# adaLN products with the weight tile stationary and the two conditions moving

## The chip, the cores and the metric

The kernel runs on one core of one Trainium2 chip. The metric is the device time of one execution in microseconds (us). Engines: PE (TensorE), DVE (VectorE), ACT (ScalarE), POOL (GpSimd) and SP (SyncE, which issues the loads of weights here). In the profile PEld stands for PE's weight loads (LDWEIGHTS) and PE for its matmuls.

## What is computed

One inference step through two trunk layers of a diffusion backbone, for 128 context tokens and 256 latent tokens of 1024 channels. Context tokens are modulated by one condition, latent tokens by another. Cut to what the change touches:

```python
mod = (jax.nn.silu(cond) @ w_ada + b_ada)[:, None, :]
sh1, sc1, gt1, sh2, sc2, gt2 = jnp.split(mod, 6, axis=-1)
h = rms_norm(x, g_mix) * (1 + sc1) + sh1
p = h @ w_in
# attention, gated linear attention (GLA) and RWKV-7 mixers on p, merged by gates
x = x + gt1 * (merged @ w_out)
h2 = rms_norm(x, g_ffn) * (1 + sc2) + sh2
x = x + gt2 * ((jax.nn.silu(gu[..., :D_FF]) * gu[..., D_FF:]) @ w_ffn_out)
```

w_ada is 1024 x 6144 in each layer, and cond is c_ctx for the context tokens and c for the latent ones. All is fp32; the large projections split their operands in a high and a low part and multiply these (L547 to L549, L1045 to L1047), the adaLN products do not.

## The kernel before

The channels lie on the 128 partitions and the 384 tokens (T) along the free axis, so that modulation is wanted as columns: mod is [128, layer, 48, 2], 48 blocks of 128 channels by two conditions. For each layer the phases are: norm and input projections, attention, GLA, RWKV, then merging, output projection and FFN. Between phases stands a barrier of all engines.

Each engine's program is written out by hand, and its instructions run in that order; engines wait for each other by semaphores. Beside the main line of a phase PE runs *side work*: a generator, side_steps, walks a plan (side_plan) of work items, and `fill(n)` runs its next n steps at the point where it stands in PE's program. Items are "ada" (adaLN: 256 of the 6144 columns of w_ada), "gate" (a 128-column gate projection, L603) and "po" (a branch's output projection, L609). An "ada" item is two steps, "po" two, "gate" four. finish(l, k) runs what is left of a plan at the end of its phase.

- Layer 0's ada items 0 to 7 run before everything else, by themselves. Items 8 to 15 of each layer stand in the plan of attention, 16 to 23 in that of GLA, and items 0 to 7 of layer 1 in the plan of layer 0's RWKV phase.
- Side work uses two PSUM banks in turn. fill_room makes PE wait until the item two places back has been emptied, by ACT (key "A") or by DVE (key "V").
- An ada item has cond (scond, 128 channels x 2 conditions for each of 8 blocks k) stationary and w_ada moving. It leaves 2 rows of 256 in PSUM; ACT copies them to a row buffer, modrow, of which there are two; turn_mod, which stands behind the item that follows, turns each row buffer into columns by two transposes; DVE adds the bias b_ada and writes mod:

```python
ins = pe.matmul(b[0:2, 0:256], scond[:, :, k], w[:, k, :], start=k == 0, stop=k == KD - 1)
...
A(modrow[0:2, j % 2, :], bank(*t)[0:2, 0:256], ACT.Copy).then_inc(*empties(*t))
...
ins = turn(b[:, 2 * i:2 * i + 2], modrow[0:2, j % 2, 128 * i:128 * i + 128])
```

- ACT and DVE empty side work in side_work(tag), called ahead of each main item: it takes all side items that PE's program finished before the item with that tag.
- The weights of all items and projections come through a ring of three buffers of 1 MB in one order (order), loaded by SP. A buffer is loaded again when its last user is done.

Names in the profile: L598 are the ada products, L499 all transposes (those of modrow have bank<-cst,modrow), L1162 ACT's copy to modrow, L1585 DVE's addition to mod, L532 the sum of squares for a norm, L713 attention's scores, L700 its output, L787 the 12 products of a GLA level, L921, L932 and L944 the narrow products of a step of the RWKV scan, L1126 and L1128 POOL's inverses.

Of the kernel before, what the change touches and what calls it, by code (L numbers as in the profile page):

```python
# [7 lines left out]
KD = D // 128  # L8
# [78 lines left out]
def step_kernel(nc, x_prompt, x_sample, cache_k, cache_v, state_gla, state_rwkv, c, c_ctx,  # L87
# [8 lines left out]
    with ExitStack() as ctx:  # L96
        offset = {}

        def sb(name, shape):
            offset[name] = nc.sbuf_base  # L100
            return ctx.enter_context(nc.sbuf_tensor(name, shape, fp32))
# [12 lines left out]
        gate = sb("gate", [128, KD, T])  # L114
# [7 lines left out]
        cst = sb("cst", [128, NCONST])  # L122
        par = sb("par", [128, L, 128])
        mod = sb("mod", [128, L, 48, 2])
        modrow = sb("modrow", [2, 2, 256])
        gtmp = sb("gtmp", [128, 2, T])
        sc1 = sb("sc1", [128, KD, 2])
        sc2 = sb("sc2", [128, KD, 2])
# [144 lines left out]
        def filled(*tag):  # L273

            return place[tag][1] + 1
# [5 lines left out]
        def emptied(*tag):  # L281

            side, n = place[tag]
            row = fills if side else items
            key = row[n][0]
            return (fill_freed if side else freed)[key], sum(1 for k, _ in row[:n + 1] if k == key)
# [180 lines left out]
        def _(pe):  # L467
# [12 lines left out]
            def fill_room():  # L480
                n = len(fills)
                return emptied(*fills[n - 2][1]) if n >= 2 else (consts_in, 16)

            def fill_item(key, *tag):
                fills.append((key, tag))
                place[tag] = 1, len(fills) - 1
                return bank(*tag)
# [9 lines left out]
            def turn(out, in_, rows=None):  # L497
                rows = rows or slice(0, in_.shape[0])
                return pe.transpose(out, in_, ident[rows, rows])  # L499
# [73 lines left out]
            h_parts = tiles(h_hi, KD), tiles(h_lo, KD)  # L573

            def turn_mod(l, j):

                pe.wait_ge(*emptied("ada", l, j))
                pe.wait_ge(*fill_room())
                b = fill_item("V", "modT", l, j)  # L580
                for i in range(2):
                    ins = turn(b[:, 2 * i:2 * i + 2], modrow[0:2, j % 2, 128 * i:128 * i + 128])
                ins.then_inc(fill_ready, 1)
                finished.append(("modT", l, j))

            def side_steps(plan):

                for n, work in enumerate(plan):
                    kind, l, j = work[0], work[1], work[-1]
                    last_of_chunk = all(chunk(later) != chunk(work) for later in plan[n + 1:])  # L590
                    pe.wait_ge(*arrived(*chunk(work)))
                    w = weights(*chunk(work))
                    pe.wait_ge(*fill_room())
                    b = fill_item("V" if kind == "po" else "A", *work)
                    if kind == "ada":

                        for k in range(KD):
                            ins = pe.matmul(b[0:2, 0:256], scond[:, :, k], w[:, k, :], start=k == 0, stop=k == KD - 1)  # L598
                            if k == 3:
                                yield  # L600
                    elif kind == "gate":
                        for k in range(KD):
                            ins = pe.matmul(b[:, 0:T], w[:, k, 128 * (j % 2):128 * (j % 2) + 128], h[:, k, :], start=k == 0, stop=k == KD - 1)  # L603
                            if k % 2 and k < KD - 1:
                                yield
                    else:
                        src = (pa[:, 0:4, :], pb[:, 4:8, :])[work[2]]
                        for k in range(4):
                            ins = pe.matmul(b[:, 0:T], w[:, k, 128 * (j % 4):128 * (j % 4) + 128], src[:, k, :], start=k == 0, stop=k == 3)  # L609
                            if k == 1:  # L610
                                yield
                    ins.then_inc(fill_ready, 1)
                    finished.append(work)
                    if last_of_chunk:
                        fill_used(*chunk(work))
                    if n and plan[n - 1][0] == "ada":
                        turn_mod(*plan[n - 1][1:])
                    yield
                if plan[-1][0] == "ada":
                    turn_mod(*plan[-1][1:])  # L620

            side = [iter(())]

# [524 lines left out]
        def _(act):  # L1148
            step, tells, empties, last, before = counting("A")
            A = act.activation  # L1150
            told_ada = []

            def side_work(*tag):

                for t in before(*tag):
                    if t[0] == "ada":
                        l, j = t[1:]
                        if len(told_ada) >= 2:
                            act.wait_ge(fill_ready, filled("modT", *told_ada[-2]))
                        told_ada.append((l, j))  # L1160
                        act.wait_ge(fill_ready, filled(*t))
                        A(modrow[0:2, j % 2, :], bank(*t)[0:2, 0:256], ACT.Copy).then_inc(*empties(*t))  # L1162
                        continue
                    kind, l, br, j = t
                    if br == 0:
                        place = mg[:, j, :]
                    elif br == 1:
                        place = gtmp[:, j % 2, :]
                        if j >= 2:
                            act.wait_ge(S["branch_merged"], told("branch_merged", l, j - 1))  # L1170
                    else:
                        place = last_gates[j]
                        act.wait_ge(fill_ready, filled("po", l, 1, 7))
                    act.wait_ge(fill_ready, filled(*t))
                    A(place, bank(*t)[:, 0:T], ACT.Sigmoid).then_inc(*empties(*t))
# [397 lines left out]
        def _(dve):  # L1573
# [3 lines left out]
            def side_work(*tag):  # L1577

                for t in before(*tag):
                    l, j = t[1], t[-1]  # L1580
                    dve.wait_ge(fill_ready, filled(*t))
                    b = bank(*t)
                    if t[0] == "modT":
                        bias = par[:, l, ROW["b_ada"] + 2 * j:ROW["b_ada"] + 2 * j + 2].unsqueeze(2).to_broadcast([128, 2, 2])
                        tt(mod[:, l, 2 * j:2 * j + 2, :], b[:, 0:4].rearrange("p (a b) -> p a b", a=2), bias, add).then_inc(*empties(*t))  # L1585
                        continue

                    dve.wait_ge(*emptied("gate", *t[1:]))
                    if t[2] == 0:
                        tt(mg[:, j, :], b[:, 0:T], mg[:, j, :], mult).then_inc(*empties(*t))  # L1590
                    else:
                        tt(gtmp[:, j % 2, :], b[:, 0:T], gtmp[:, j % 2, :], mult).then_inc(*empties(*t))
                        dve.wait_ge(*last())
                        tt(mg[:, j, :], mg[:, j, :], gtmp[:, j % 2, :], add).then_inc(*tells("branch_merged"))
# [548 lines left out]
```

## Time and profile before

| | us |
|---|---|
| median of 3 runs | 2234.6 (2234.24 to 2237.12) |
| the profiled execution | 2236.58 |
| its span, first to last instruction | 2234.8 |
| PE busy | 1952.0 (87%) |
| DVE, ACT, POOL busy | 1055.9, 838.4, 283.0 |
| mean granted clock of PE | 0.923 of full speed |

The profile is of one execution. Rows of groups give the line, engine, operation, output<-inputs, shapes and the number of records, then the busy time of all and the mean of one in ns. A fp32 matmul of this kernel leaves two records (and two weight loads), a transpose one.
### The profile page before, as it was taken

What the parts mean: (1) busy time and instruction counts of PE and PEld (TensorE: products, weight loads), DVE (VectorE), ACT (ScalarE), POOL (GpSimd) and SP (SyncE); (2) the same over time, 40 slices, a digit from 0 to 9 for tenths busy, and PEclk for the clock granted to TensorE, in tenths of its full rate; (3) what the DMA queues carried; (4) which work ended last, traced back from release to release, by engine and by line L of the source; (5) the groups of instructions that cost most, each with busy time, mean ns of one, the idle gap of its engine ahead of it and who ended that gap; (6) DMA issues with size and microseconds to landing.
All of it is one profiled execution on the core that took longest, in us unless ns stands there. A gap on an engine that the chain in (4) does not pass through costs nothing.

```text
span 2234.8 us, 32380 instructions
## 1 busy us (share of the span) xinstructions
PE 1952.0 (87%) x13395; PEld 1551.7 (69%) x13395; DVE 1055.9 (47%) x1939; ACT 838.4 (38%) x1408; POOL 283.0 (13%) x550
## 2 busy tenths in 40 slices
PE   6899998967985798999989989897787668899998
PEld 2799445634554598999979965464444557799998
DVE  0336427754565544343342544384466645533433
ACT  1533533253333535333253345324324334533322
POOL 2000000015555000000000000000553520000000
PEclk9999999978996799999999999998887569999999
DMA  7433333202130143443433423323101003344342
GB/s 255 132 116 104 100 113 123 95 24 76 58 114 20 33 151 94 121 125 105 128 112 122 125 82 114 107 92 99 57 2 57 2 1 102 111 114 132 107 119 85
DMA packets 267769, 214.07 MB, mean 96 GB/s; under 512 B 7209, under 2 KB 259400, under 8 KB 267368
## 3 DMA queue, kind: packets, MB, share of 16 engines
q1 hardware_dynamic: 264640, 204.39, 30.1%
q0 software_dynamic: 2736, 7.54, 1.1%
q8 instruction: 107, 1.75, 0.3%
q14 instruction: 38, 0.31, 0.0%
q10 hardware_dynamic: 248, 0.07, 0.0%
HBM read 209.10 MB, written 2.88 MB: 95 GB/s over the span
## 4 chain that ended last, share of the span: by engine, by line
PE 70%; DVE 11%; ACT 7%; POOL 7%; issue 3%; DMA 1%; DVEq 0%; ACTq 0%; POOLq 0%
PE bank L547 10%; PE bank L548 10%; PE bank L549 10%; PE bank L603 8%; PE bank L598 7%; POOL cst L1128 4%; POOL lora L1126 3%; PE bank L1047 3%; PE bank L1046 3%; PE bank L1045 3%; PE bank L609 2%; PE bank L787 2%; PE bank L499 1%; ACT h L1192 1%; PE bank L834 1%
## 5 line engine op out<-in xcount | busy, mean ns | idle before, releaser
L549 PE MATMUL bank<-scr_rounded 128*128 128x384 f32 (+1 forms) x1312 | 442.0, 337 | 0.0
L603 PE MATMUL bank<-h,ring 128*128 128x384 f32 x640 | 249.0, 538 | 21.8 <-DVEq L337 17.9
L547 PE MATMUL bank<-scr_rounded 128*128 128x384 f32 x672 | 230.2, 343 | 26.0 <-DVE scr_rounded L1605 24.2
L549 PEld LDWEIGHTS bank<-scr_rounded 128*128 128x128 f32 (+1 forms) x1312 | 247.9, 189 | 1.0
L548 PE MATMUL bank<-scr_rounded 128*128 128x384 f32 x672 | 227.7, 339 | 0.0
L1600 DVE TENSOR_TENSOR scr_rounded<-ring,scr_rounded 128x2048 fp32r<-128x2048 f32 (+1 forms) x64 | 136.1, 2126 | 177.6 <-ACT scr_rounded L1183 176.8
L547 PE MATMUL bank<-scr_rounded,gate_rounded 128*128 128x384 f32 (+1 forms) x640 | 214.6, 335 | 4.4 <-DVE scr_rounded L1600 4.4
L548 PE MATMUL bank<-scr_rounded,gate_rounded 128*128 128x384 f32 (+1 forms) x640 | 214.3, 335 | 0.0
L603 PEld LDWEIGHTS bank<-h,ring 128*128 128x128 f32 x640 | 126.5, 207 | 119.4 <-issue 54.8
L598 PE MATMUL bank<-ring,scond 128*2 128x256 f32 x768 | 182.1, 391 | 19.5 <-DVE mg L1590 6.0
L1600 DVE TENSOR_TENSOR scr_rounded<-ring,gate_rounded 128x2048 fp32r<-128x2048 f32 (+3 forms) x64 | 130.2, 2034 | 106.0 <-ACT gate_rounded L1183 105.4
L1183 ACT ACTIVATE scr_rounded<-ring 128x2048 fp32r<-128x2048 f32 (+1 forms) x64 | 114.0, 1781 | 145.2 <-PE bank L549 74.8
L1183 ACT ACTIVATE gate_rounded<-ring 128x2048 fp32r<-128x2048 f32 (+3 forms) x64 | 109.2, 1707 | 146.4 <-PE bank L549 85.7
L547 PEld LDWEIGHTS bank<-scr_rounded 128*128 128x128 f32 x672 | 128.9, 192 | 32.0 <-issue 26.5
L598 PEld LDWEIGHTS bank<-ring,scond 128*2 128x2 f32 x768 | 62.7, 87 | 124.2 <-issue 40.4
L1128 POOL TENSOR_TENSOR cst<-cst,lora 128x30 f32<-128x30 f32 (+14 forms) x240 | 128.2, 534 | 18.8
L548 PEld LDWEIGHTS bank<-scr_rounded 128*128 128x128 f32 x672 | 128.8, 192 | 0.3
L547 PEld LDWEIGHTS bank<-scr_rounded,gate_rounded 128*128 128x128 f32 (+1 forms) x640 | 119.4, 187 | 6.0 <-DVE scr_rounded L1600 5.1
L1126 POOL TENSOR_TENSOR lora<-cst 128x30 f32<-128x30 f32 (+14 forms) x240 | 120.1, 500 | 18.2
L548 PEld LDWEIGHTS bank<-scr_rounded,gate_rounded 128*128 128x128 f32 (+1 forms) x640 | 119.3, 186 | 1.0
L2097 DVE TENSOR_TENSOR arena<-bank,arena 128x384 f32<-128x384 f32 x44 | 24.5, 558 | 177.1 <-PE bank L549 175.6
L609 PE MATMUL bank<-arena,ring 128*128 128x384 f32 x256 | 94.2, 511 | 2.8 <-DVE mod L1585 1.6
(358 smaller groups left out, 3253.7 us busy)
## 6 DMA issues: line engine op xcount, KB each, us to landing
ring<-in_w_in_dram SPq DMA_DIRECT2D x56, 1024.0 KB, 5.3
ring<-in_w_ada_dram SPq DMA_DIRECT2D x48, 1024.0 KB, 5.3
ring<-in_w_ffn_in_dram SPq DMA_DIRECT2D x88, 512.0 KB, 5.1
ring<-in_w_ffn_out_dram SPq DMA_DIRECT2D x32, 704.0 KB, 4.6
ring<-in_w_out_dram SPq DMA_DIRECT2D x8, 1024.0 KB, 5.1
ring<-in_w_po_a_dram SPq DMA_DIRECT2D x4, 1024.0 KB, 6.3
ring<-in_w_po_b_dram SPq DMA_DIRECT2D x4, 1024.0 KB, 5.4
ring<-in_w_po_c_dram SPq DMA_DIRECT2D x4, 1024.0 KB, 6.3
```

The source lines that it names most:

```text
L547: pe.matmul(o, w_hi[:, k, :], right[0][k], start=k == 0, stop=False)
L548: pe.matmul(o, w_hi[:, k, :], right[1][k], start=False, stop=False)
L549: ins = pe.matmul(o, w_lo[:, k, :], right[0][k], start=False, stop=k == nk - 1)
L598: ins = pe.matmul(b[0:2, 0:256], scond[:, :, k], w[:, k, :], start=k == 0, stop=k == KD - 1)
L603: ins = pe.matmul(b[:, 0:T], w[:, k, 128 * (j % 2):128 * (j % 2) + 128], h[:, k, :], start=k == 0, stop=k == KD - 1)
L609: ins = pe.matmul(b[:, 0:T], w[:, k, 128 * (j % 4):128 * (j % 4) + 128], src[:, k, :], start=k == 0, stop=k == 3)
L1045: pe.matmul(b[:, 0:T], w_hi[:, k, :], ff_hi[n], start=n == 0, stop=False)
L1046: pe.matmul(b[:, 0:T], w_hi[:, k, :], ff_lo[n], start=False, stop=False)
L1126: gp.tensor_tensor(t, W[:, i + 1:32, i:i + 1].to_broadcast([128, more, i]), over(W[:, i, 0:i], more), mult).then_inc(*step())
L1128: gp.tensor_tensor(W[:, i + 1:32, 0:i], W[:, i + 1:32, 0:i], t, add).then_inc(*(step() if i < 30 else tells("rw_inv")))
L1183: A(shaped(whi[m % 2], name, j), weights(l, name, j), ACT.Copy).then_inc(*tells("w_hi"))
L1600: tt(shaped(wlo[m % 2], name, j), weights(l, name, j), value(shaped(whi[m % 2], name, j)), sub).then_inc(*tells("w_lo"))
```

## The change

The weight tile becomes the stationary operand and the condition the moving one. Each item is then 2 x 8 instructions, which leave the two blocks of 128 channels as columns in PSUM, in the layout that the transposes had left there. modrow, turn_mod and ACT's copy are gone; the item's bank is emptied by DVE's addition, which is the same instruction as before. The step of the generator now ends after the first block of 128 channels, so that an item is still two steps of equal length.

```diff
-        modrow = sb("modrow", [2, 2, 256])
...
-            def turn_mod(l, j):
-
-                pe.wait_ge(*emptied("ada", l, j))
-                pe.wait_ge(*fill_room())
-                b = fill_item("V", "modT", l, j)
-                for i in range(2):
-                    ins = turn(b[:, 2 * i:2 * i + 2], modrow[0:2, j % 2, 128 * i:128 * i + 128])
-                ins.then_inc(fill_ready, 1)
-                finished.append(("modT", l, j))
...
-                    b = fill_item("V" if kind == "po" else "A", *work)
+                    b = fill_item("A" if kind == "gate" else "V", *work)
                     if kind == "ada":
 
-                        for k in range(KD):
-                            ins = pe.matmul(b[0:2, 0:256], scond[:, :, k], w[:, k, :], start=k == 0, stop=k == KD - 1)
-                            if k == 3:
+                        for i in range(2):
+                            for k in range(KD):
+                                ins = pe.matmul(b[:, 2 * i:2 * i + 2], w[:, k, 128 * i:128 * i + 128], scond[:, :, k], start=k == 0, stop=k == KD - 1)
+                            if i == 0:
                                 yield
...
-                    if n and plan[n - 1][0] == "ada":
-                        turn_mod(*plan[n - 1][1:])
                     yield
-                if plan[-1][0] == "ada":
-                    turn_mod(*plan[-1][1:])
...
-                    if t[0] == "ada":
-                        l, j = t[1:]
-                        if len(told_ada) >= 2:
-                            act.wait_ge(fill_ready, filled("modT", *told_ada[-2]))
-                        told_ada.append((l, j))
-                        act.wait_ge(fill_ready, filled(*t))
-                        A(modrow[0:2, j % 2, :], bank(*t)[0:2, 0:256], ACT.Copy).then_inc(*empties(*t))
-                        continue
...
-                    if t[0] == "modT":
+                    if t[0] == "ada":
                         bias = par[:, l, ROW["b_ada"] + 2 * j:ROW["b_ada"] + 2 * j + 2].unsqueeze(2).to_broadcast([128, 2, 2])
```

The order of PE's instructions at the start of the program (L598 are the ada products, dve_emptied_fill and act_emptied_fill the waits for a bank of side work), before:

```order
L598 MATMUL bank<-ring,scond 2x256 [waits consts_in,w_arrived1]
L598 MATMUL bank<-ring,scond 2x256 x7
L499 MATMUL bank<-cst,modrow 128x2 [waits act_emptied_fill]
L499 MATMUL bank<-cst,modrow 128x2
L598 MATMUL bank<-ring,scond 2x256 [waits act_emptied_fill,w_arrived2]
L598 MATMUL bank<-ring,scond 2x256 x7
L499 MATMUL bank<-cst,modrow 128x2 [waits dve_emptied_fill,act_emptied_fill]
L499 MATMUL bank<-cst,modrow 128x2
```

and after the change, where the products stand in L588:

```order
L588 MATMUL bank<-scond,ring 128x2 [waits consts_in,w_arrived1]
L588 MATMUL bank<-scond,ring 128x2 x15
L588 MATMUL bank<-scond,ring 128x2 [waits dve_emptied_fill,w_arrived2]
L588 MATMUL bank<-scond,ring 128x2 x15
L588 MATMUL bank<-scond,ring 128x2 [waits dve_emptied_fill,w_arrived0]
L588 MATMUL bank<-scond,ring 128x2 x15
```

Items now follow each other on PE with no transposes between them, and the wait for ACT has become one for DVE.

PE in the first levels of GLA in layer 0 (L787 are the 12 products of a level), before:

```order
L598 MATMUL bank<-ring,scond 2x256 [waits act_emptied_fill,w_arrived2]
L598 MATMUL bank<-ring,scond 2x256 x7
L499 MATMUL bank<-cst,modrow 128x2 [waits dve_emptied_fill,act_emptied_fill]
L499 MATMUL bank<-cst,modrow 128x2
L787 MATMUL bank<-scr 128x128 [waits dve_emptied,gla_z]
L787 MATMUL bank<-scr 128x128 x5
L787 MATMUL bank<-scr 128x128 [waits dve_emptied]
L787 MATMUL bank<-scr 128x128 x5
L598 MATMUL bank<-ring,scond 2x256 [waits act_emptied_fill,w_arrived0]
L598 MATMUL bank<-ring,scond 2x256 x7
```

and after, with the level's products in L773:

```order
L588 MATMUL bank<-scond,ring 128x2 [waits dve_emptied_fill,w_arrived2]
L588 MATMUL bank<-scond,ring 128x2 x15
L773 MATMUL bank<-scr 128x128 [waits dve_emptied,gla_z]
L773 MATMUL bank<-scr 128x128 x5
L773 MATMUL bank<-scr 128x128 [waits dve_emptied]
L773 MATMUL bank<-scr 128x128 x5
L588 MATMUL bank<-scond,ring 128x2 [waits dve_emptied_fill,w_arrived0]
L588 MATMUL bank<-scond,ring 128x2 x15
```

Each item keeps its level; an item is 16 instructions in place of 8 and two transposes.

## Rows read from the trace of the kernel before

**Rows 1.** The page: busy time by engine, and the chain that ended last.
```profile
PE 1952.0 (87%) x13395; PEld 1551.7 (69%) x13395; DVE 1055.9 (47%) x1939; ACT 838.4 (38%) x1408; POOL 283.0 (13%) x550
...
PE 70%; DVE 11%; ACT 7%; POOL 7%; issue 3%; DMA 1%; DVEq 0%; ACTq 0%; POOLq 0%
PE bank L547 10%; PE bank L548 10%; PE bank L549 10%; PE bank L603 8%; PE bank L598 7%; POOL cst L1128 4%; POOL lora L1126 3%; PE bank L1047 3%; PE bank L1046 3%; PE bank L1045 3%; PE bank L609 2%; PE bank L787 2%; PE bank L499 1%; ACT h L1192 1%; PE bank L834 1%
```

**Rows 2.** Groups by line: busy us, mean ns | idle before, releasers.
```profile
L598 PE MATMUL bank<-ring,scond 128*2 128x256 f32 x768 | 182.1, 391 | 19.5 <-DVE mg L1590 6.0 <-DVEq L337 5.0 <-issue 4.4
...
L1162 ACT ACTIVATE modrow<-bank 2x256 f32<-2x256 f32 x48 | 17.9, 372 | 120.6 <-PE bank L598 117.2 <-DVE scr L1906 3.4
```

**Rows 3.** Chain of waits from the start: start us, us, what.
```profile
38.63 3.63 PE bank L598 x16
42.34 0.38 ACT modrow L1162
42.85 3.63 PE bank L598 x16
...
60.28 5.18 PE bank L532 x16
```

**Rows 4.** Timeline of PE, three runs of transposes: start us, us, engine, line.
```profile
14.98 4.82 PE L499 MATMUL bank<-cst,mg 128*128 128x128 f32 x24
...
467.04 0.72 PE L499 MATMUL bank<-cst,scr 64*128 64x64 f32 x8
...
2225.27 2.81 PE L499 MATMUL bank<-cst,x 128*128 128x128 f32 x24 [0.93 <-DVEq L337]
```

**Rows 5.** Stretches of first products: PE, PEld, DVE, ACT, POOL, PEclk, DMA share, GB/s.
```profile
24.30:29.30 5.00, 4.99 (x12) 1.49 (x13) 0.00 (x0) 0.00 (x0) 0.00 (x0) 0.50 1.05 333
29.40:59.30 29.90, 27.54 (x131) 10.75 (x129) 0.97 (x6) 2.67 (x8) 0.00 (x0) 1.00 0.76 245
```

**Rows 6.** Timeline of PE in the levels of GLA, layer 0.
```profile
367.75 3.62 PE L598 MATMUL bank<-ring,scond 128*2 128x256 f32 x16
371.30 0.28 PE L499 MATMUL bank<-cst,modrow 2*128 2x2 f32 x2
371.51 1.61 PE L787 MATMUL bank<-scr 64*128 64x128 f32 x24
373.05 3.62 PE L598 MATMUL bank<-ring,scond 128*2 128x256 f32 x16
...
389.04 2.82 PE L609 MATMUL bank<-arena,ring 128*128 128x384 f32 x8 [0.81 <-DVE mod L1585]
391.79 1.61 PE L787 MATMUL bank<-scr 64*128 64x128 f32 x24
393.33 2.85 PE L609 MATMUL bank<-arena,ring 128*128 128x384 f32 x8
```

**Rows 7.** RWKV scans of layer 0: timeline of PE, then stretches.
```profile
625.51 1.89 PE L598 MATMUL bank<-ring,scond 128*2 128x256 f32 x8
627.33 0.73 PE L932 MATMUL bank<-cst,scr 64*64 64x64 f32 x16
...
688.06 1.15 PE L932 MATMUL bank<-cst,scr 64*64 64x64 f32 x16 [1.84 <-issue]
...
624.50:654.10 29.60, 27.65 (x227) 13.61 (x226) 14.19 (x50) 5.42 (x19) 26.07 (x46) 1.00 0.69 214
684.40:702.60 18.20, 11.98 (x150) 9.11 (x148) 13.00 (x45) 4.38 (x14) 12.71 (x28) 0.50 0.00 1
```

**Rows 8.** Timeline of PE and DVE in a pair of attention blocks.
```profile
253.57 0.92 PE L713 MATMUL bank<-scr,arena 64*128 64x384 f32 x4
254.42 2.85 PE L603 MATMUL bank<-h,ring 128*128 128x384 f32 x8
256.55 0.42 DVE L1738 TENSOR_SCALAR scr<-scr,small 128x384 f32<-128x384 f32 x1
257.10 0.82 PE L499 MATMUL bank<-cst,scr 128*128 128x128 f32 x6
```

**Rows 9.** Stretch of GLA levels without an ada item, same columns.
```profile
388.00:410.00 22.00, 21.19 (x158) 13.85 (x156) 21.03 (x44) 4.88 (x7) 0.00 (x0) 1.00 0.15 49
```

More of the change, by code:

```diff
@@ L1150, in _ @@
             A = act.activation
-            told_ada = []
             def side_work(*tag):
                 for t in before(*tag):
-                    if t[0] == "ada":
-                        l, j = t[1:]
-                        if len(told_ada) >= 2:
-                            act.wait_ge(fill_ready, filled("modT", *told_ada[-2]))
-                        told_ada.append((l, j))
-                        act.wait_ge(fill_ready, filled(*t))
-                        A(modrow[0:2, j % 2, :], bank(*t)[0:2, 0:256], ACT.Copy).then_inc(*empties(*t))
-                        continue
                     kind, l, br, j = t
```

## The prediction, made before the changed kernel ran

> **What bounds the kernel now.** I read the page's shares and its chain first: TensorE (PE) is busy for 87% of the span and makes 70% of the chain that ended last; the adaLN products alone (L598) are 7% of that chain [rows 1]. So what happens to PE's time counts wherever the chain runs through PE, and I then looked at the four places in which these products run, for what ends last there.
>
> The groups by line give unit times [rows 2]. Each instruction in fp32 leaves two records. An adaLN item (8 instructions) is 16 records. The timeline gives an item as one piece of 3.61 to 3.62 us, its two transposes of modrow behind it (0.28 us shown, 0.21 to the next start) [rows 6]. Start to start, a half item (8 records) takes 1.82 us [rows 7], so about 216 ns a record once 0.1 us for the break is taken off. 48 items are 48 x 3.83 = 184 us of PE.
>
> - *Start (24.3 to 60 us).* Nothing but these products runs. PE waits between items for ScalarE's copy to modrow (0.37 us each [rows 2]), so an item is 4.2 us from start to start [rows 3].
> - *Attention.* In a pair of blocks PE runs scores, a piece of side work, transposes. VectorE and ScalarE need until 256.97 for scores begun at 253.57, and the transposes start at 257.10 [rows 8]: with a gate piece of 2.85 us PE and the others just meet, with an adaLN item of 3.62 us PE is the later by some 0.7 us.
> - *GLA.* Each level is L787 (1.61 us, 1.54 to the next start) and one piece: 5.3 us with an adaLN item, 4.3 us with a 2.85 us piece [rows 6]. In the levels with the shorter pieces VectorE is busy 21.03 of 22 us [rows 9]. So about 4.2 us is the floor of a level, whatever PE saves.
> - *RWKV scans of layer 0.* Narrow products (64 columns) alternate with half items of 1.89 us [rows 7].
>
> **The change part by part.** An item becomes 16 instructions, 32 records, each with a stationary tile of 128x128 and 2 moving columns. Gone are 96 transposes, 48 copies on ScalarE and the wait for them. VectorE's 48 additions stay as they are and now empty the product itself; a wait for them stands where PE waited for ScalarE. Behind that wait on PE are all later products of the stage; VectorE reaches it before the PE needs the bank again in the orders shown, and where it was late (0.81 us at 389.0 [rows 6]) it was late before. I cost this at nothing, up to 0.8 us a time if that cover fails. The ring's 1 MB loads keep their places; with DMA at a share of 0.76 in the first stage [rows 5] a shorter item could wait for its weights there, see the first rival.
>
> *A record at full clock.* With 2 columns there is nothing to hide the loading of 128 columns of weights. The nearest row is the run of eight transposes that move 64 columns against a 128-column stationary tile [rows 4]: 0.72 us, of which a lone record is 0.28, so (0.72 - 0.28) / 7 = 63 ns from start to start. The upper bound is that of 128 moving columns, (2.81 - 0.28) / 23 = 110 ns [rows 4], the lower one half of it, 55 ns, since 64 columns could fill no more than that. I take 63, since that row is limited by the load: an item is 32 x 63 + two breaks of 0.1 = 2.2 us against 3.83, 1.6 less. The Trainium skill (TensorE: Matmul & The Clock Gate, section "LDWEIGHTS (loading the stationary operand)") gives columns / 1.2, so 107 ns for 128 columns: by it an item would be an estimated 3.6 us and nearly all of the gain at full clock would be gone. The 63 ns row is shorter than that rule, so the row decides.
>
> *A record at half clock.* Some 57 of the 63 ns should be the load itself and double with the clock: 115 to 120 ns, I take 115. The upper bound is the slow run of 128-column transposes at 15 us, 24 in 4.82 us, 200 ns each [rows 4]. An item is 32 x 115 + 0.2 = 3.9 us: as much as the old one at full clock.
>
> *Which clock it is.* This decides everything. A new record moves 2 columns where an old one moves 256: 216 ns x 2/256, under 2 ns in 63. The rows show what held the clock. In the RWKV scans with a half item between the narrow products the granted clock is 1.00 (2.4 GHz); the same scans without anything between them run at 0.50 (1.2 GHz), though PE is busy for 12.0 of 18.2 us and weights are being loaded for half of it (9.1 us) [rows 7]. The old items at 24.3 us began at 0.50 and went on at 1.00 [rows 5], though their stationary tile has only 2 columns: moving columns raised it, not the width of the tile. Items of 2 moving columns should therefore look idle, and I expect the clock to fall to 1.2 GHz behind each run of them, and to stay there until wide products have run for some us. The Trainium skill (same page, "Part 1: The HAM clock gate") says that the gate follows how busy PE has been and does not say whether loading weights counts; that is the first rival.
>
> The sum, at the expected clock:
>
> 1. Start: 256 records x 115 ns = 29.4 us against 35.8 (24.3 to 60.1): -6. The 16 records of L532 behind them (5.18 us at full clock [rows 3]) begin at half, 640 ns each; 7.5 us if the clock rises after some ten of them: +2.5. Sum -3.5, bounds -6 and -1.
> 2. Attention, each layer: the opening fill is 48 records, about 40 at full clock and then half, 4.2 us against 5.3, and the ten records of L657 behind it (384 moving columns, 0.32 us each as in L532 [rows 3]) at half clock cost 2 to 3 more: +1. Of six later items some three leave the clock up and gain 1.1 each (VectorE allows no more: 3.4 us from score to transpose); three bring it down, so that the next scores, transposes and gate piece (0.92, 0.82 and 2.85 us [rows 8]) run partly at half, +2 to +3 each. -3.3 + 6.6 + 1 = +4 a layer, bounds -3 and +11.
> 3. GLA, each layer: a level at full clock 4.2 against 5.3, at half 3.9 + 3.2 = 7.1, so -1.1 or +1.8. First item -1, its following L499/L773 at half +0.8, three levels in a row one fast and two slow +2.5, first wide level after them at half +2; then a lone level -1, two in a row +0.8, the output products L798/L802 begun at half +2, last item -1: +5 a layer, bounds -5 and +12.
> 4. RWKV, layer 0: 16 half items at 1.95 against 1.83, +2; the narrow products between them at half as at 688 us, where 16 records of L932 take 1.15 us against 0.73 [rows 7]: +0.9 a scan step, 4.5 steps, +4; two steps until the clock is back, +2; transposes gone, -2. +6, bounds -2 and +10.
>
> -3.5 + 8 + 10 + 6 = +20.5. The profiled execution took 2236.58 us with a span of 2234.8 (1.8 us around it); the median of the three timed runs is 2234.6, 2.0 below it. Put on the median: 2255.
>
> **The rivals.** *The clock holds* (weight loads count as activity, or the pieces around suffice). Then each item is 2.2 us. Start: the first us are at half clock all the same, afterwards the ring limits: 1 MB at 333 GB/s [rows 5], about 3.1 us an item, -10 in all. Attention: -1.1 for six items and -2 for the opening, -8.5 a layer. GLA: eight items at -1.1, -9 a layer (VectorE's 4.2 us is the bound). RWKV: 8 items of which VectorE and POOL (7% of the chain, L1126 and L1128 [rows 1]) let some 1.0 each through, -8. -10 - 17 - 18 - 8 = -53, from 2234.6: 2182. For it: no row shows weights loaded for long without moving columns, so that this is excluded by none. Against it: the scans at 0.50 with loads half the time [rows 7]. It decides from the point at which a run of items leaves the granted clock at 1.00.
>
> *The change saves nothing on PE*: a load of 128 fp32 rows takes the upper bound of 110 ns at both clocks. An item is 3.7 us, as before, and the clock falls all the same: the sum gets the fast items' gains back, +8: about 2262. The skill's rule above would end here.
>
> *The falls are cheap*: the clock comes back within one piece, since every second piece is wide. Attention and GLA come to nothing or -3 a layer, RWKV +2, start -3.5: 2230 to 2237, about 2234, no measurable difference.
>
> **How the numbers follow.** The forecast has 0.57, its own range 2238 to 2275 (nearly the ends of its terms, which won't all fall together). The clock holds: 0.28, 2172 to 2200. Nothing saved: 0.05. Cheap falls: 0.10. For 8 in 10 the range must reach into the first rival: 2172 to 2275. A measurement of this kernel can tell some 0.2% (4.5 us) from no change. Faster by more: 0.28 and a little of the cheap falls, 0.30. Within: 0.08. Slower: 0.62.
>
> **What would show it.** PEclk (slices and stretches) at 0.5 in 25 to 60 us and under 0.9 in the GLA levels with adaLN items; a piece of 32 records of 3.7 us there and of 2.1 us where the clock is still up; the gate and score pieces behind items lengthened. VectorE's additions to mod wait for the products themselves, and the 48 copies of L1162 (17.9 us [rows 2]) are gone. If PEclk is 1.00 in all adaLN runs, the reading of the clock is wrong and the first rival's sum holds; if 32 records take over 3.4 us at 1.00, the price of the load is wrong.

## The result, and the profile after

The changed kernel takes 2386.1 us (median; 2365.7 to 2390.1) against 2234.4: 1.065 times the time of before, 95% interval 1.062 to 1.069. It is 152 us slower; the forecast had been 20 slower, and the range ended at 2275. In this document a ratio and its interval leave out runs over 1.5% above a kernel's fastest, which only two programs had.

The page of the changed kernel: busy time, and the granted clock of PE in 40 slices of the span.

```profile
PE 2114.8 (89%) x14067; PEld 1806.2 (76%) x14067; DVE 1057.8 (44%) x1939; ACT 823.2 (34%) x1360; POOL 282.8 (12%) x550
...
PEclk6799888758587589999999988867688757999999
...
PE bank L588 11%; PE bank L546 10%; PE bank L548 10%; PE bank L547 10%; PE bank L593 9%; POOL cst L1114 3%; POOL lora L1112 3%; PE bank L1032 3%; PE bank L1031 3%; PE bank L1033 3%; PE bank L773 2%; PE bank L599 2%; ACT h L1169 1%; PE bank L498 1%; PE bank L699 1%
```

PE is busy for 163 us more than in [rows 1], PEld for 254 us more, DVE for 2 more. In the kernel before the same clock row reads:

```profile
PEclk9999999978996799999999999998887569999999
```

The adaLN products have gone from 7% of the chain to 11%. The groups by line, of the changed kernel and then of before (busy us, mean ns | idle before):

```profile
L588 PE MATMUL bank<-scond,ring 128*128 128x2 f32 x1536 | 274.9, 314 | 14.3 <-DVE mg L1567 6.0 <-DVEq L336 5.0 <-issue 3.3
L593 PE MATMUL bank<-h,ring 128*128 128x384 f32 x640 | 271.2, 577 | 20.7 <-DVEq L336 17.9 <-DMA ring<-in_w_in_dram 2.9
L773 PE MATMUL bank<-scr 64*128 64x128 f32 x672 | 61.0, 345 | 0.0
L1562 DVE TENSOR_TENSOR mod<-bank,par 128x4 f32<-128x4 f32 x48 | 7.7, 161 | 163.8 <-PE bank L588 163.4
```

```profile
L603 PE MATMUL bank<-h,ring 128*128 128x384 f32 x640 | 249.0, 538 | 21.8 <-DVEq L337 17.9 <-DMA ring<-in_w_in_dram 2.2 <-ACT mg L1175 0.9
L787 PE MATMUL bank<-scr 64*128 64x128 f32 x672 | 45.0, 280 | 0.0
```

The adaLN products themselves cost 275 us of busy time against 182 [rows 2], and products that the change doesn't touch became dearer too: a gate record takes 577 ns in place of 538 on average, a record of a GLA level 345 in place of 280. The stretches of the start answer to [rows 5] (PE, PEld, DVE, ACT, POOL, PEclk, DMA share, GB/s):

```profile
24.30:29.30 5.00, 5.00 (x25) 5.00 (x25) 0.00 (x0) 0.00 (x0) 0.00 (x0) 0.50 0.85 267
29.40:59.30 29.90, 29.90 (x141) 29.90 (x142) 0.81 (x5) 0.00 (x0) 0.00 (x0) 0.50 0.46 147
```

Here PE loads weights without a pause, and the granted clock is 0.50 (1.2 GHz) where it was 1.00. 141 records in 29.9 us are 212 ns each. The timeline of PE in the levels of GLA answers to [rows 6]:

```profile
414.08 2.93 PE L773 MATMUL bank<-scr 64*128 64x128 f32 x24
416.94 6.99 PE L588 MATMUL bank<-scond,ring 128*128 128x2 f32 x32
423.86 2.94 PE L773 MATMUL bank<-scr 64*128 64x128 f32 x24
426.72 6.99 PE L588 MATMUL bank<-scond,ring 128*128 128x2 f32 x32
433.64 2.94 PE L773 MATMUL bank<-scr 64*128 64x128 f32 x24
436.50 3.96 PE L599 MATMUL bank<-arena,ring 128*128 128x384 f32 x8
440.39 1.61 PE L773 MATMUL bank<-scr 64*128 64x128 f32 x24
```

A level with an item is 9.8 us from start to start (416.94 to 426.72) against 5.3: the item 6.9 in place of 3.6, the level's own products 2.9 in place of 1.6. Inside the first wide piece behind them the clock comes back, and the next level is at its old 1.61 us.

From the times at which the same PE record of either trace starts, the stages compare like this:

| Stretch (layer) | before, us | after, us | longer by |
|---|---|---|---|
| start to L532/L531 (0) | 60.1 | 77.9 | 17.8 |
| to attention's L657/L643, with the opening fill (0) | 167.6 | 171.6 | 4.0 |
| to GLA's L736/L722 (0) | 111.7 | 127.1 | 15.4 |
| GLA (0) | 123.0 | 159.9 | 36.9 |
| RWKV, to the first L547/L546 behind it (0) | 321.8 | 344.3 | 22.5 |
| to attention's L657/L643 (1) | 528.0 | 534.6 | 6.6 |
| attention (1) | 111.9 | 125.1 | 13.2 |
| GLA (1) | 123.3 | 159.8 | 36.5 |
| the rest, with no adaLN item in it | 687.4 | 687.9 | 0.5 |

All of the loss lies in the stretches that hold adaLN items. Adding up PE's records of both traces, each from its start to the next start and without idle time, gives the second split: the items (in the kernel before with the transposes of modrow) went from 190 to 271 us, all other records from 1762 to 1844, PE's idle time shrank by 9. So about half of the loss is the items' own length, and half is their neighbours, which took longer at half clock.

What a record costs is read from the same starts: inside items the distance is 112 ns where the granted clock is 1.00 and 213 ns where it is 0.50. Of 1489 such distances 918 lay wholly or partly at half clock.

### The profile page after: what moved, and what is told of

Read it like the earlier page. It is cut to its first block, busy times and chain, and to the rows that moved or that the text cites. A ratio compares the mean times of both kernels' runs of the same rounds, so it can differ in the third digit from the quotient of the medians.

```text
span 2388.2 us, 33583 instructions
## 1 busy us (share of the span) xinstructions
PE 2114.8 (89%) x14067; PEld 1806.2 (76%) x14067; DVE 1057.8 (44%) x1939; ACT 823.2 (34%) x1360; POOL 282.8 (12%) x550
## 4 chain that ended last, share of the span: by engine, by line
PE 73%; DVE 9%; POOL 7%; ACT 6%; issue 3%; DMA 1%; DVEq 0%; ACTq 0%; POOLq 0%
PE bank L588 11%; PE bank L546 10%; PE bank L548 10%; PE bank L547 10%; PE bank L593 9%; POOL cst L1114 3%; POOL lora L1112 3%; PE bank L1032 3%; PE bank L1031 3%; PE bank L1033 3%; PE bank L773 2%; PE bank L599 2%; ACT h L1169 1%; PE bank L498 1%; PE bank L699 1%
## 5 line engine op out<-in xcount | busy, mean ns | idle before, releaser
L588 PEld LDWEIGHTS bank<-scond,ring 128*128 128x128 f32 x1536 | 271.9, 278 | 27.3 <-issue 24.9
L593 PE MATMUL bank<-h,ring 128*128 128x384 f32 x640 | 271.2, 577 | 20.7 <-DVEq L336 17.9
L588 PE MATMUL bank<-scond,ring 128*128 128x2 f32 x1536 | 274.9, 314 | 14.3 <-DVE mg L1567 6.0
L546 PE MATMUL bank<-scr_rounded 128*128 128x384 f32 x672 | 230.3, 343 | 26.1 <-DVE scr_rounded L1582 24.2
L593 PEld LDWEIGHTS bank<-h,ring 128*128 128x128 f32 x640 | 138.1, 226 | 131.3 <-issue 74.8
L547 PE MATMUL bank<-scr_rounded 128*128 128x384 f32 x672 | 227.6, 339 | 0.0
L546 PE MATMUL bank<-scr_rounded,gate_rounded 128*128 128x384 f32 (+1 forms) x640 | 215.3, 336 | 4.4 <-DVE scr_rounded L1577 4.4
L547 PE MATMUL bank<-scr_rounded,gate_rounded 128*128 128x384 f32 (+1 forms) x640 | 215.1, 336 | 0.0
L546 PEld LDWEIGHTS bank<-scr_rounded 128*128 128x128 f32 x672 | 128.7, 192 | 32.4 <-issue 26.5
L547 PEld LDWEIGHTS bank<-scr_rounded 128*128 128x128 f32 x672 | 128.8, 192 | 0.3
L546 PEld LDWEIGHTS bank<-scr_rounded,gate_rounded 128*128 128x128 f32 (+1 forms) x640 | 120.0, 188 | 6.0 <-DVE scr_rounded L1577 5.1
L547 PEld LDWEIGHTS bank<-scr_rounded,gate_rounded 128*128 128x128 f32 (+1 forms) x640 | 119.9, 187 | 1.0
```

The costliest lines, as they stand in the source:

```text
L546: pe.matmul(o, w_hi[:, k, :], right[0][k], start=k == 0, stop=False)
L547: pe.matmul(o, w_hi[:, k, :], right[1][k], start=False, stop=False)
L588: ins = pe.matmul(b[:, 2 * i:2 * i + 2], w[:, k, 128 * i:128 * i + 128], scond[:, :, k], start=k == 0, stop=k == KD - 1)
```

## The experiments

Theory A, formed on these two traces: a record is limited by the load of its 128 fp32 columns, at 112 ns at full and 213 ns at half clock, so an item at full clock is no shorter than the old one; and the clock falls because of the few moving columns. Rivals: the clock falls through the weight loads or the waits (B), load and moving add up (C), the neighbours' half clock is most of the loss (D), the phases' losses hang together (E). Two came up later, on the price of a load (G) and on a wait (H).

### 128 moving columns

In all experiments of this kind scond is repeated by an access pattern with step 0, so that m columns move; DVE reads two of them. Everything else is the changed kernel.

```diff
-ins = pe.matmul(b[:, 2 * i:2 * i + 2], w[:, k, 128 * i:128 * i + 128], scond[:, :, k], ...)
+m = 128
+ins = pe.matmul(b[:, m * i:m * i + m].rearrange("p (a b) -> p a b", b=2), w[:, k, 128 * i:128 * i + 128],
+                scond[:, :, k].unsqueeze(1).to_broadcast([128, m // 2, 2]), ...)
```

> The changed kernel, but with 128 moving columns in each adaLN product (the two conditions repeated 64 times; only two of the columns are used), weights still stationary. Theory A (a record is limited by the load of 128 fp32 columns, 111 ns at full clock and 213 at half, and the clock falls because so few columns move): 128 columns move in the shadow of the load, a record stays at 110 to 112 ns, an item at 3.6 us, and PEclk is 1.00 in the adaLN stretches; then only the transposes and the copy's wait are gone, 4.6 us at the start and some 0.2 us for each other item where PE is the later: about 2221 us, 2212 to 2232. Rival B (the clock falls through the many weight loads of 128 columns, or the waits, not through the moving columns): PEclk stays at 0.5 in the start and the time at 2365 to 2390. Rival C (load and moving do not overlap): about 218 ns a record at full clock, an item 7 us, time 2350 or more.

Measured: 2227.1 us, 0.9965 of before (0.9952 to 0.9977), within the range expected. 64 times as many columns go through PE, and it takes 159 us less than the changed kernel. The stretches of the start, and two levels of GLA:

```profile
24.30:29.30 5.00, 5.00 (x27) 5.00 (x27) 0.00 (x0) 0.00 (x0) 0.00 (x0) 0.57 1.05 331
29.40:59.30 29.90, 29.90 (x245) 28.18 (x244) 4.33 (x14) 3.19 (x2) 0.00 (x0) 1.00 0.87 278
```

```profile
366.59 1.61 PE L774 MATMUL bank<-scr 64*128 64x128 f32 x24
368.13 3.84 PE L589 MATMUL bank<-scond,ring 128*128 128x128 f32 x32
371.90 1.61 PE L774 MATMUL bank<-scr 64*128 64x128 f32 x24
```

The clock is at 1.00 with the same stationary tiles, the same number of loads and the same waits: rival B falls. A record is 112 ns as with 2 moving columns at full clock, so the 128 columns move wholly beside the load: rival C falls. An item is 3.77 us (368.13 to 371.90). A level is 5.31 us against 5.29 of before (one old item and the two transposes): in GLA the form gains nothing even at full clock. What it does gain is the start, where no copy by ACT is waited for (5 us at the norm), and 3 us in attention of each layer.

### 256 moving columns

> The same with 256 moving columns. It lengthens the items about as the half clock does, but should leave the clock up. Theory A: 213 to 216 ns a record at PEclk 1.00 in all adaLN runs, an item 6.9 us, neighbours at their lengths of before; so +19 us at the start and 3 us for each of the 40 other items where PE is the later, about +130 us in all: 2350 to 2375 us, and by as much as it stays below 2386 the neighbours at half clock had cost more. If the neighbours' half clock were the greater part of the loss (rival D), this kernel would be below 2320. Rival B: PEclk 0.5 here too, 400 ns a record and over 2450 us.

Measured: 2387.1 us, 1.068 of before (1.066 to 1.069). The granted clock of the start is that of before, and the neighbours have their old length:

```profile
29.40:59.30 29.90, 29.90 (x138) 26.02 (x137) 0.65 (x4) 0.00 (x0) 0.00 (x0) 1.00 0.43 141
```

```profile
425.94 1.61 PE L774 MATMUL bank<-scr 64*128 64x128 f32 x24
427.48 7.25 PE L589 MATMUL bank<-scond,ring 128*128 128x256 f32 x32
434.67 1.61 PE L774 MATMUL bank<-scr 64*128 64x128 f32 x24
```

A record is 218 ns: now the moving of 256 columns is the limit. At full clock an item is 7.2 us, some 3.4 more than the old one with its transposes (3.83), and 48 x 3.4 = 163 us, less what PE waited for in before, is what the kernel lost. The expectation was 12 to 37 us too low, since it took 3 us an item and only where PE is the later. It also was a poor test of D: here all 48 items are long, in the changed kernel only those at half clock. That the two totals agree is chance; the changed kernel's split into 81 us of items and 82 of neighbours rests on the traces' records alone. By the same adding up the kernel with 256 columns has 349 us of items and 1764 of all other records, which is 159 and 2 more than before. What this run shows is that items twice as long cost their full length nearly everywhere, so PE's side work is on the path in all four stages.

### 2 moving columns in the start alone, and in GLA alone

```diff
+m = 2 if l == 0 and j < 8 else 128      # the start
+m = 2 if 16 <= j < 24 else 128          # GLA
```

> 128 moving columns everywhere but in the first eight items, which run alone at the start with 2 as in the changed kernel. Theory A: PEclk 0.50 through 23 to 78 us, 256 records at 213 ns in 54.7 us, and nothing lost behind the norm: 2221 + 24 = about 2245 us, 2235 to 2255. Rival E: more than 30 us above m128.

Measured: 2252.7 us, 25.6 above the kernel with 128 columns, 24 expected. The granted clock of the start:

```profile
24.30:77.00 52.70, 52.70 (x249) 52.70 (x249) 1.14 (x7) 3.19 (x2) 0.00 (x0) 0.50 0.52 167
```

> 128 moving columns everywhere but in the items of GLA (16 to 23 of each layer), which have 2 as in the changed kernel. Theory A: the loss is local to the phase; GLA is 36.6 us longer in each layer than before, as in the changed kernel, and PEclk returns to 1.00 behind it: 2221 + 2 x 38 = about 2297 us, 2285 to 2310. Rival E (the losses of the phases hang together through the weight ring and the side work's plan): less than half of that, or some of it in attention and RWKV.

Measured: 2265.7 us for the two shorter of four runs, 1.013 of before (1.012 to 1.015). That is 39 above the kernel with 128 columns and 19 below the expected range. The four runs were 2265, 2267, 2307 and 2307 us, so the same program lost 39 or 80 us. The longer runs had the lower mean granted clock, 0.885 against 0.897; why a run gets the one or the other was not settled. The trace is of one of the short runs. In it GLA is 22.5 and 20.9 us longer than before in the two layers, where the changed kernel's was 36.9 and 36.5: the expectation had the changed kernel's loss here, and this trace shows little more than half of it.

Rival E is answered by the stages of the two traces. With 2 columns in the start alone, the start is 24 us longer than in the second trace of the kernel with 128 columns (from the last experiment), the stretch from there to attention 3, and each other stage lies within 1 us of it. With 2 columns in GLA alone, each other stage lies within 3 us of the first trace of that kernel. So the losses of the phases don't hang together, beyond the 3 us of products that follow the start while the clock is still down.

### 64 and 32 moving columns

> As the run with 128 moving columns (weights stationary, 128 columns), but 64 move. Theory A: the record's price stays 111 ns at full and 213 at half clock; the time then tells only the clock. Half the moving columns for the same time should let it fall in some of the item runs: 2235 to 2300 us, PEclk in the start between 0.5 and 1.0. Rival B (columns don't matter for the clock below 256): as 128 columns, 2227 us. Rival C (load and moving add up): shorter by 50 ns a record than with 128.

> The same with 32 moving columns. Theory A: the record still takes 111 or 213 ns; the clock stays at 0.50 in the start as with 2 columns, 256 records in 54.7 us, and the whole time is 2350 to 2390 us. If 32 columns already hold the clock, 2227 us; the two between them place where the clock is lost.

Measured: 2296.0 us with 64 columns (1.026 of before, 1.024 to 1.028) and 2348.4 with 32 (1.049, 1.047 to 1.051; 2 us under the expected range). The time with 64 columns is within its range, but the clock of the start was expected between 0.5 and 1.0 and is 0.50. The second stretch of the start, first with 64 and then with 32 columns:

```profile
29.40:59.30 29.90, 29.90 (x142) 29.90 (x142) 0.81 (x5) 0.00 (x0) 0.00 (x0) 0.50 0.46 147
```

```profile
29.40:59.30 29.90, 29.90 (x142) 29.90 (x142) 0.81 (x5) 0.00 (x0) 0.00 (x0) 0.50 0.44 142
```

In both, records have the distances of the changed kernel, 112 ns at full and 213 at half clock; only their share at half clock differs: 918 of 1489 with 2 columns, 666 with 32, 471 with 64, 61 with 128. The time rises with that share: 2386, 2348, 2296, 2227 us. So up to 128 the number of moving columns acts on the time through the clock alone. The places differ too: with 64 columns the start is 17.6 us longer than before, as with 2, and RWKV 12.5, but GLA only 2.5 and 7.1.

### Half of the stationary columns

```diff
+m = 64
+for n, k in enumerate([0, *range(KD)]):
+    c = 64 if n else 128
+    ins = pe.matmul(b[0:c, ...], w[:, k, 128 * i:128 * i + c], ..., start=n < 2, stop=n in (0, KD))
```

The products with 64 stationary columns leave out half of the channels, so this kernel does not compute the right modulation; it is there for its time alone.

> 64 moving columns, and the stationary tile cut to 64 of its 128 columns in 16 of the 18 products of an item (one product of each block keeps 128, so that all partitions are written); half of the adaLN channels are left out of the sum. It asks what a load of half the columns costs, and what short items are worth while the clock is up. Theory A (price of a load goes by its columns, 64 columns in some 55 to 60 ns): 4 x 111 + 32 x 57 = 2.3 us an item at PEclk 1.00. If 64 moving columns hold the clock, the sum of the prediction's first rival then applies (start -10, attention -8.5 and GLA -9 a layer, RWKV -8): about 2185 us, 2175 to 2205. If they don't hold it, 4.5 us an item at half clock and 2250 to 2300. Rival G (a load has a fixed price of about 110 ns whatever its columns): 36 records, 4.0 us an item at full clock, 2245 us or more.

Measured: 2207.2 us, 0.988 of before (0.986 to 0.990), 2 us above the range expected.

```profile
29.40:59.30 29.90, 25.40 (x264) 20.84 (x262) 5.24 (x15) 6.13 (x7) 0.00 (x0) 0.99 0.98 316
```

```profile
363.24 2.95 PE L590 MATMUL bank<-scond,ring 128*128 128x64 f32 x36
366.12 1.61 PE L775 MATMUL bank<-scr 64*128 64x128 f32 x24
367.66 2.95 PE L590 MATMUL bank<-scond,ring 128*128 128x64 f32 x36
```

(The timeline counts both shapes of product as one.) A record with 64 stationary columns is 58 to 59 ns from start to start, half of 112: the price of a load goes by its columns, and rival G falls. The four records with 128 columns and the changes between the shapes cost more than expected (107 to 205 ns each), so that an item is 2.9 us and not 2.3. And here the clock is at 0.99 with 64 moving columns, in records of 58 ns; in the same stretch it was at 0.50 with as many columns in records that load 128. The first rival's sum, -53 us, was for items of 2.2 us at full clock; with 2.9 us the kernel gains 30. By stage, in the trace: start 9.8 us (10 in the sum), attention with its opening fill 3.5 a layer (8.5), GLA 2.8 a layer (9), RWKV 6.6 (8). In the start the ring is near its limit, as that rival had it: 316 GB/s at a DMA share of 0.98, and PE is busy for 25.4 of 29.9 us.

### Where VectorE's addition stands

In the kernel with 128 columns GLA was 1.5 us longer than before in layer 0, though its levels had their old length. The timelines of the kernel before and then of that kernel, around the first item of GLA:

```profile
358.61 3.61 PE L598 MATMUL bank<-ring,scond 128*2 128x256 f32 x16 [3.00 <-DVE mg L1590]
...
361.21 0.96 DVE L1773 TENSOR_TENSOR scr<-scr,arena 128x768 f32<-128x768 f32 x1 [2.28 <-ACT scr L1342]
...
364.83 1.09 PE L499 MATMUL bank<-cst,scr 128*128 128x128 f32 x8 [2.60 <-DVE scr L1774]
```

```profile
350.74 3.81 PE L589 MATMUL bank<-scond,ring 128*128 128x128 f32 x32 [3.01 <-DVE mg L1569]
...
354.59 0.16 DVE L1564 TENSOR_TENSOR mod<-bank,par 128x4 f32<-128x4 f32 x1 [3.53 <-PE bank L589]
354.67 0.95 DVE L1752 TENSOR_TENSOR scr<-scr,arena 128x768 f32<-128x768 f32 x1
...
358.28 1.09 PE L498 MATMUL bank<-cst,scr 128*128 128x128 f32 x8 [3.73 <-DVE scr L1753]
```

In the kernel before DVE waits for ACT only and starts its products 2.6 us behind the item's start. Now its addition to mod stands ahead of them and waits for the item; the products start 3.9 us behind the item's start, and PE stands still for 3.73 us in place of 2.60. The experiment moves the addition behind the four products, and runs beside the kernel with 128 columns once more:

```diff
-side_work("khT", l, 0)
+side_work("ada", l, 16)
 dve.wait_ge(S["gla_exps"], told("gla_exps", l, 1))
```

> The kernel with 128 moving columns once more, beside the next one, to be compared on the same chip: 2227 us, 2222 to 2232, the ratio to before 0.9952 to 0.9977 as it was.

> The kernel with 128 moving columns, but VectorE empties the first adaLN item of GLA (one in each layer) behind its own two pairs L1752/L1753 and not ahead of them. Theory H (the changed wait costs time: VectorE, which the order of before let go on while ScalarE emptied the item, now stands still until PE is through with it, and PE's transposes for the level's keys wait for VectorE in turn; 3.73 us from item to transposes against 2.60 before): the wait goes back to about 2.6 us, 1.3 us a layer, in all -2.6 us against the kernel with 128 columns, so about 2224.5. Rival: the transposes wait for ScalarE's or the item's end all the same, and nothing changes (within 1 us). A difference this small may drown in the runs' spread; the gap in the trace decides.

Measured: 2228.4 us for the kernel with 128 columns (0.9962, 0.9950 to 0.9974). With the addition moved, four of five runs took 2219.7 to 2225.5 us, 2220.6 as their median (0.9936, 0.9923 to 0.9948). The fifth took 4788 us at a granted clock of 1.00; nothing here explains it, and it is left out. The first product of transposes of layer 1 in GLA, with 128 columns and then with the addition moved:

```profile
1442.78 1.09 PE L498 MATMUL bank<-cst,scr 128*128 128x128 f32 x8 [3.73 <-DVE scr L1753]
```

```profile
1435.14 1.09 PE L498 MATMUL bank<-cst,scr 128*128 128x128 f32 x8 [2.40 <-DVE scr L1753]
```

The wait is 2.40 us in place of 3.73, 1.33 less, as theory H has it. The gain of the whole kernel is 6 us by the ratios, and uncertain by some 4, so the times don't tell it from the 2.6 expected; the wait does. The same place in layer 0, with 128 columns and then with the addition moved:

```profile
357.25 1.97 PE L498 MATMUL bank<-cst,scr 128*128 128x128 f32 x8 [3.73 <-DVE scr L1753]
359.15 3.52 PE L760 MATMUL bank<-gate,scr 128*64 128x128 f32 x32
```

```profile
349.53 6.68 PE L589 MATMUL bank<-scond,ring 128*128 128x128 f32 x32 [3.00 <-DVE mg L1569]
356.05 1.04 PE L498 MATMUL bank<-cst,scr 128*128 128x128 f32 x8
357.02 1.97 PE L760 MATMUL bank<-gate,scr 128*64 128x128 f32 x32
```

Here the clock differs as well. With 128 columns the half clock fell on the products behind the wait, which took 5.4 us. With the addition moved it fell on the item, which took 6.5 us in place of 3.8 and filled the time in which PE would have waited; the products ran at full clock, 2.9 us. The wait is no sufficient reason for the half clock: behind the same 3.73 us the first product ran at full clock in the first trace of the kernel with 128 columns (358.28, 1.09 us) and in layer 1 above. That the moved addition brings the other clock in layer 0 is therefore not shown. By the traces' stages GLA gained 3.5 us in layer 0 and 1.4 in layer 1. RWKV of layer 0 is 2.3 shorter, but the two traces of the kernel with 128 columns differ by 2.1 there, so this is no gain. This kernel is the fastest of the study among those that compute everything: 14 us, 0.64%, under before.

## Why the prediction was wrong

**The sign and the clock** came out as forecast. PEclk is 0.50 in the whole start and falls at items of all stages; the 48 copies of ACT are gone, and DVE waits for the products themselves (163.4 us before the additions of L1562). Both rivals on the clock fell: it doesn't hold with 2 moving columns, and its falls aren't cheap. Three steps failed.

**The price of a record was the step that failed most.** The prediction says that the "nearest row is the run of eight transposes that move 64 columns against a 128-column stationary tile". That is a misreading: the row says 64*64, a stationary tile of 64 rows and 64 columns [rows 4]. Its 63 ns are the price of half a tile, as the run with 64 stationary columns confirms with 58 to 59. The row with the right tile stood beside it, 24 records of 128*128 in 2.81 us, 110 ns each, and was taken for the upper bound only; measured are 112. The same with half clock: 115 ns was worked out by doubling the wrong row, while the 24 records of 128*128 at 15 us gave 200; measured are 213. So an item is 3.6 us at full clock, where 2.2 was forecast, and 6.9 at half, where 3.9 was. The Trainium skill (TensorE: Matmul & The Clock Gate, section "LDWEIGHTS (loading the stationary operand)") gives columns / 1.2, an estimated 107 ns for 128 columns and 53 for 64. The prediction turned this down because of the misread row. The traces agree with it at full clock to within a tenth, with 112 and 58 ns, and at half clock they show twice as much, 213 ns. The rival that the change saves nothing on PE had the price at full clock right (110 ns, a chance of 0.05). It took the same 110 ns at half clock, and so its 2262 us are 124 too few.

**The terms of the sum**, with what they came to:

| Term | forecast | measured | with 112 and 213 ns in the forecast's working |
|---|---|---|---|
| start | -3.5 | +19.2 | 256 x 213 ns = 54.5 against 35.8, +2.5 behind it: +21 |
| attention, a layer | +4 | +18 | nothing is gained by items at full clock; those at half cost 3 each, and neighbours |
| GLA, a layer | +5 | +37 | a level at half clock is 6.9 + 2.9 = 9.8 against 5.3, not 7.1 |
| RWKV | +6 | +22.5 | 14 of 16 half items at half clock, 3.5 against 1.8 us each: +23 |

(Attention is given with its opening fill: 2.6 and 15.4 in layer 0, 5.0 and 13.2 in layer 1. 19.2 is the start with what the norm and the first projections behind it lose; 1.6 us more lie in layer 1's projections.) The places and the causes were the right ones, each slow item with slow neighbours behind it; the start follows from the price within 2 us, and in RWKV the half items' own length is the whole term.

**How long the clock stays down was the second.** In GLA the forecast had one of three levels in a row at full clock. In the trace none of the three is: they take 7.7 us (409.20 to 416.94), 9.8 and 9.8 against 5.3, and at 416 to 436 us PEclk is 0.50 throughout. Together they lose 11.4 us, where the forecast had 2.5. The timeline shows the first item of the three:

```profile
409.20 4.95 PE L588 MATMUL bank<-scond,ring 128*128 128x2 f32 x32
```

The kernels with 2, 32, 64 and 128 moving columns show that the losses grow with the share at half clock. Why the clock stays down for longer than forecast isn't shown; whether the longer items add to it is open.

**The wait on VectorE, costed at nothing, was the third.** "VectorE reaches it before the PE needs the bank again" looked at PE's next use of the bank, not at what stands behind the addition on VectorE itself. At GLA's first item four products of DVE stand there, and PE waits for them: 1.1 us more per layer at full clock (3.73 against 2.60). The experiment with the addition moved took the wait back to 2.40. In the changed kernel PE's wait there is 3.72 us, behind an item of 5.1 us that runs at half clock for much of its length.

```profile
404.72 1.97 PE L498 MATMUL bank<-cst,scr 128*128 128x128 f32 x8 [3.72 <-DVE scr L1751]
```

**The range** missed because the bounds of the price were written down and then not carried through. With 200 ns the start alone is 51.2 us against 35.8, +15, where the term's bounds were given as -6 and -1; the GLA and attention terms had been cut in the same way.

## What to carry to other kernels

Which operand is stationary decides what is paid: a 128-column fp32 tile costs 112 ns to load and about as much to move, so making it the stationary one saves nothing, and with 2 columns to move nothing hides the load. Then the clock: products that load weights and move only 2 columns leave PE busy by its records and at 1.2 GHz by its granted clock, and here their neighbours paid as much as they did. If such a form is wanted for its layout, move as many columns as the load hides (here 128, at no cost in PE time), and look at what stands behind every wait that changes engines.

## What the runs showed of the hardware that had not been expected

- Weight loads with 2 moving columns didn't raise the clock: 52.7 us with PEld busy throughout stayed at 0.50. Padding to 128 columns, useless for the result, brought 1.00 and made the kernel 159 us faster.
- The number of moving columns alone doesn't tell the clock. 64 columns in records of 213 ns stayed at 0.50 in the start; 64 columns with half the load, in records of 58 ns, were at 0.99 in the same stretch.
- The load's price at half clock is 1.9 times that at full clock (213 to 112 ns), so a slow item is as long as one with 256 moving columns at full clock (6.9 and 7.2 us).
- A change between products of 128 and 64 stationary columns cost up to some 100 ns a record (records of 150 to 205 ns next to others of 58).
- One program had runs 42 us apart (2265 and 2307), with 2 moving columns in GLA alone, at mean granted clocks of 0.897 and 0.885. Two traces of the kernel with 128 columns differ too: the first products behind the wait in GLA of layer 0 took 1.09 us in one and 1.97 in the other.
